# The compressed keys' first layer: 32 full-height products in place of 128 half-height ones

## The chip, the cores and the metric

The kernel runs on one core of a Trainium2 chip, all in float32, as one launch. The time is the device time of that launch in microseconds; lower is better. Five instruction queues run side by side and meet only at semaphores: TensorE (PE, matrix products and transposes into PSUM), VectorE (DVE), ScalarE (ACT), GpSimd (POOL) and SyncE (SP), of which SP only issues transfers here.

## What is computed

Two transformer blocks over 256 tokens of width 1024. The second block mixes a gated recurrence with a sparse attention, then runs a layer that picks 16 experts per head and token out of 16,384, and a gate. The change is in one piece of the sparse attention, the compressed keys and values: each of two key/value groups has 256 tokens of 64 features; blocks of 32 tokens, one every 16 tokens, are each flattened, given a position term and sent through a two-layer network.

```python
def compress(a, pe, w1, w2):          # a: groups x tokens x 64
    c = a.reshape(B, G, T // 16, 16, 64)
    blk = jnp.concatenate([c[:, :, j:j + n_cmp] for j in range(2)], axis=3)   # 15 blocks of 32 tokens
    blk = (blk + pe).reshape(B, G, n_cmp, 32 * 64)
    return jax.nn.gelu(blk @ w1) @ w2                                         # w1: 2048 x 64, w2: 64 x 64
kc = rmsnorm_2(compress(k_cmp, cmp_pe[0], cmp_w1[0], cmp_w2[0]), k_gain[0])
vc = compress(v_cmp, cmp_pe[1], cmp_w1[1], cmp_w2[1])
```

So the first layer is, for keys and for values (`kv`), a sum over 32 token places `j` of a 64x64 weight times the 15 tokens `16 m + j` of each group.

## The kernel before, in words

Everything stays in on-chip memory. Weights come from `wall` in 35 units of 2 MB, through a ring of three slots (`ring`); SP issues unit after unit, each when the unit that had its slot has been used (semaphore `unit_used`). One program for each engine is written out by hand, and the order in it is the order of execution. PE takes the units in the order `nq`, `nk`, `nv`, `hf`, `hq`, `cmp`, `hi`, `hg`, `wp0`, `wp1`, then the expert layer's. The function `project` runs a unit's products in eight parts and puts small steps of the attention and of the recurrence between the parts.

Around the change this is the order:

- PE (lines 679 to 771): the projections `nq`, `nk`, `nv`; two transposes of the normed keys and queries (`turn_nsa`); the projections `hf` and `hq` with the window attention of the first 128 tokens between their parts; then the unit `cmp` (line 740); then `project("hi")`, whose part 0 starts with `turn_keys` (line 752, eight transposes), part 1 with `within_chunks` (line 763), part 2 with `compressed` (lines 770 and 771, the second layer), part 4 with `turn_compressed`, part 6 with `compressed_scores`.
- DVE: `nsa_normed(t)` (line 1665) writes the normed, feature-major keys and values `nT3` for each half of the tokens; then four additions (line 1704) write `pe0` and `pe1`, the tokens with the position term of the block's first and second 16 places; then the attention's and the recurrence's steps, of which the last (line 1735) releases `turn_keys` through `recur_ready`.
- ACT: copies the projections out of PSUM (line 1080), does the exponentials of the recurrence (lines 1244 to 1249), then takes the first layer's sums out of PSUM through the gelu (lines 1254 and 1255), then moves the turned keys (line 1261).
- POOL: makes masks, issues the load of `post_g` (line 462) once block 1 is done, waits for `intra_moved` (line 471), and from there on gathers the experts' rows (line 489), 256 gathers of 1 MB.

In the unit `cmp` the group `g` is the half of the 128 partitions: features 0 to 63 of group 0 lie on partitions 0 to 63, those of group 1 on 64 to 127. Each product uses a 64x64 weight on one half of the array and 15 columns, each 16 tokens apart. There are 2 groups x 2 (`kv`) x 32 places = 128 products. A float32 product stands in the trace as two records, so these are 256.

PE's next instruction after the last of the 128 waits for `recur_ready`; ACT's next instruction waits for `unit_used` of `cmp`.

Of the kernel before, what the change touches and what calls it, by code (L numbers as in the profile page):

```python
# [19 lines left out]
ALU = mybir.AluOpType  # L20
ACT = mybir.ActivationFunctionType
AX = mybir.AxisListType.X

P = 128
SEQ = 256
# [50 lines left out]
def ring_slot(u):  # L76
# [15 lines left out]
        ("nq_g", 1), ("nk_g", 3), ("pe", 2 * CMP_LEN), ("cmp_w2", 2 * DH)]  # L92
COL_AT, NCOL = {}, 0
for _name, _width in COLS:
# [12 lines left out]
        "o_std", "nsa_sums", "nsa_std", "nsa_scaled", "nsa_turned", "nsa_normed", "cmp_in", "hid_made",  # L107
# [68 lines left out]
def two_blocks(nc, x, wall, cols, rows, lambdas, sub_keys, peer_uv, out):  # L176
    with ExitStack() as ctx:
# [42 lines left out]
        class at2:  # L220
# [16 lines left out]
            pe0, pe1 = sm[:, D:D + HALF], sm[:, D + HALF:2 * D]  # L237
# [26 lines left out]

        head_mask = small2[:, 1512:1520]
# [134 lines left out]
        def _(pool):  # L400
# [61 lines left out]
            pool.dma_start(post_g[:, :], rows[1:2, :].broadcast_to([P, D])).then_inc(s["rows_loaded"], 16)  # L462

# [31 lines left out]
        def _(pe):  # L495
# [570 lines left out]
        def _(act):  # L1066
# [184 lines left out]
            act.wait_ge(s["unit_used"], UNIT_AT["cmp"] + 1)  # L1251
            for g in range(NKV):
                half = slice(g * DH, (g + 1) * DH)
                nc.scalar.activation(hid_k[half, g * 16:g * 16 + NCMP], hid_psum[half, 0:NCMP], ACT.Gelu_apprx_tanh)
                ins = nc.scalar.activation(hid_v[half, :].rearrange("p (r m) -> p r m", r=REP)
# [886 lines left out]
```

## Time and profile before

| | us |
|---|---|
| median of 3 runs | 1183.0 |
| lowest, highest | 1182.2, 1183.18 |
| the profiled execution's own time | 1184.88 |
| its span in the profile | 1183.1 |
| mean granted TensorE clock in it | 0.974 of full |

The profile is one execution. Its views used here are the page (shares of the span, and the span in 40 slices), the chain of work that ended last (each step followed back to what released it), the timeline (instructions in order of time, neighbours merged, with the idle time before them and who ended it) and windows (busy time of each engine in a stretch, with the granted clock). The granted clock is 1.00 at 2.4 GHz and 0.50 at 1.2 GHz. The duration of a matmul record includes its way through the array, so what a row of records costs is read from the chain, where neighbours do not overlap.

### The profile page before, as it was taken

The page shows a single profiled execution, that of the slowest core. Times are in us where ns is not written, and L with a number is a line of the kernel's source. Part 1 is how long each engine was busy: PE and PEld are TensorE (multiplying, and loading weights), DVE is VectorE, ACT ScalarE, POOL GpSimd, SP SyncE. Part 2 cuts the span into 40 slices and gives each one's busy share as a digit, 9 for nine tenths or more (in the row PEclk, how much of TensorE's full clock was granted, in tenths as well). Part 3 has the DMA queues.
Part 4 walks back from the last instruction along what each step waited for, and adds up shares of the span by engine and source line. Part 5 has one row for each costly group of instructions (what it writes and reads, how often), then busy time and mean ns, then how long its engine had stood idle before and what let it go on. Part 6 is the DMA issues. An engine that isn't in the chain of part 4 may idle for free.

```text
span 1183.1 us, 9911 instructions
## 1 busy us (share of the span) xinstructions
PE 1036.0 (88%) x3363; PEld 558.0 (47%) x3363; DVE 641.5 (54%) x1446; ACT 390.8 (33%) x1019; POOL 310.2 (26%) x310
## 2 busy tenths in 40 slices
PE   6999899999999997988898997977699777777777
PEld 5887458544797554543344443322244222222223
DVE  2515345312540326877575655766776677667442
ACT  0133245211451123444433323423442432333222
POOL 3000000012000001244363433544354434444420
PEclk9999999999996998999999998999999999999999
DMA  7335322234531217699999999999999999999980
GB/s 276 143 142 213 142 99 115 88 139 165 195 143 72 107 71 284 219 369 423 420 422 420 421 421 422 420 419 420 421 393 420 421 419 420 421 420 420 420 346 18
DMA packets 43442, 346.96 MB, mean 293 GB/s; under 512 B 4832, under 2 KB 4960, under 8 KB 6016
## 3 DMA queue, kind: packets, MB, share of 16 engines
q0 software_dynamic: 37200, 269.63, 55.7%
q1 hardware_dynamic: 6192, 76.71, 17.1%
q8 instruction: 26, 0.43, 0.1%
q14 instruction: 24, 0.20, 0.0%
HBM read 345.27 MB, written 1.05 MB: 293 GB/s over the span
## 4 chain that ended last, share of the span: by engine, by line
PE 57%; DMA 30%; DVE 6%; ACT 4%; issue 2%; SPq 0%; POOL 0%; POOLq 0%; DVEq 0%
DMA spare<-in_peer_uv,small 17%; PE pp L940 15%; PE pp L524 7%; DMA gl<-in_peer_uv,small 7%; PE pp L552 5%; PE pp L548 4%; PE pp L534 3%; DMA ring<-in_wall 3%; PE pa L890 3%; DMA sm<-in_peer_uv,small 3%; PE pp L1032 2%; PE pp L659 2%; PE pp L679 2%; PE pp L637 2%; PE pa L740 2%
## 5 line engine op out<-in xcount | busy, mean ns | idle before, releaser
L1342 ACT ACTIVATE small<-small 128x2 f32<-128x2 f32 x128 | 26.0, 203 | 396.7 <-DVE small L1958 396.5
L940 PE MATMUL pp<-ga,diag 128*128 128x512 f32 x132 | 68.2, 641 | 34.3 <-ACT diag L1356 34.3
L1356 ACT ACTIVATE diag<-ident,small 128x128 f32<-128x128 f32 x256 | 88.7, 393 | 4.3
L940 PE MATMUL pp<-kT,diag 128*128 128x512 f32 x132 | 65.4, 618 | 27.3 <-ACT diag L1356 27.2
L940 PE MATMUL pp<-xc_rg,diag 128*128 128x512 f32 x132 | 65.5, 620 | 27.1 <-ACT diag L1356 27.1
L524 PE MATMUL pp<-hT,ring 128*128 128x256 f32 x384 | 85.8, 386 | 2.7 <-DMA ring<-in_wall 2.7
L524 PEld LDWEIGHTS pp<-hT,ring 128*128 128x128 f32 x384 | 74.6, 194 | 13.5 <-issue 3.0
L940 PE MATMUL pp<-tail,diag 128*128 128x512 f32 x116 | 56.6, 610 | 22.9 <-ACT diag L1356 22.3
L489 POOL DMA_INDIRECT xc_rg<-in_peer_uv,small x33 | 37.0, 1121 | 148.3 <-issue 77.8
L449 POOL IOTA tail<- 128x256 int32 x1 | 0.3, 341 | 248.3 <-DVE xs L1618 248.3
L1348 ACT ACTIVATE small<-small 128x1 f32<-128x1 f32 x256 | 61.4, 287 | 5.3
L940 PE MATMUL pp<-spare,diag 128*128 128x512 f32 x132 | 62.7, 598 | 0.0
L940 PE MATMUL pp<-ig,diag 128*128 128x512 f32 x132 | 62.4, 595 | 0.0
L940 PE MATMUL pp<-gl,diag 128*128 128x512 f32 x132 | 62.1, 592 | 0.0
L548 PE MATMUL pp<-ring,hT 128*128 128x512 f32 x128 | 61.3, 626 | 0.0
L940 PEld LDWEIGHTS pp<-ga,diag 128*128 128x128 f32 x132 | 24.2, 197 | 75.0 <-ACT diag L1356 54.1
L552 PE MATMUL pp<-hT,ring 128*128 128x256 f32 x256 | 58.1, 381 | 0.0
L1958 DVE CUSTOM_DVE_ANT_0 xc_rg<-xc_rg 128x1024 f32<-128x1024 f32 x33 | 40.4, 1225 | 30.2 <-DMA xc_rg<-in_peer_uv,small 30.0
L489 POOL DMA_INDIRECT ga<-in_peer_uv,small x33 | 37.5, 1136 | 71.3 <-PE pp L940 70.7
L1958 DVE CUSTOM_DVE_ANT_0 gl<-gl,xc_rg 128x1024 f32<-128x1024 f32 x33 | 40.4, 1224 | 27.5 <-DMA gl<-in_peer_uv,small 27.5
L1958 DVE CUSTOM_DVE_ANT_0 spare<-spare,xc_rg 128x1024 f32<-128x1024 f32 x33 | 40.5, 1226 | 27.3 <-DMA spare<-in_peer_uv,small 27.1
L890 PE MATMUL pa<-ring,hT 128*128 128x512 f32 (+1 forms) x112 | 52.4, 563 | 2.9 <-DMA ring<-in_wall 2.9
(384 smaller groups left out, 1888.3 us busy)
## 6 DMA issues: line engine op xcount, KB each, us to landing
ring<-in_wall SPq DMA_DIRECT2D x35, 2048.0 KB, 7.8
xs<-in_x SPq DMA_DIRECT2D x2, 512.0 KB, 3.8
post_g<-in_rows POOLq DMA_DIRECT2D x2, 512.0 KB, 8.7
lt<-in_sub_keys SPq DMA_DIRECT2D x1, 1024.0 KB, 6.4
out<-xs SPq DMA_DIRECT2D x4, 256.0 KB, 4.8
xc_rg<-in_peer_uv,small POOLq DMA_INDIRECT x33
gl<-in_peer_uv,small POOLq DMA_INDIRECT x33
ga<-in_peer_uv,small POOLq DMA_INDIRECT x33, 12.6
```

The lines of the kernel that those rows point to most:

```text
L489: nc.gpsimd.indirect_dma_start(out=rows_uv[page_of(g)], out_offset=None, in_=peer_uv, in_offset=bass.IndirectOffsetOnAxis(ap=experts[:, g: ...
L524: ins = nc.tensor.matmul(buf[:, c, :], w[:, k, c * P:(c + 1) * P], h3[:, k, :], start=(k == 0), stop=(k == KC - 1))
L534: ins = nc.tensor.matmul(buf[:, t, 0:width], h3[:, k, t * P:(t + 1) * P], w[:, k, 0:width], start=(k == 0), stop=(k == KC - 1))
L548: ins = nc.tensor.matmul(buf[:, t, :], h3[:, k, t * P:(t + 1) * P], w[:, k, :], start=(k == 0), stop=(k == KC - 1))
L552: ins = nc.tensor.matmul(flat[:, c, :], w[:, k, c * P:(c + 1) * P], h3[:, k, :], start=(k == 0), stop=(k == KC - 1))
L637: ins = nc.tensor.matmul(bufs[c][:, t, :], gl3[:, k, t * P:(t + 1) * P], wo[c][:, k, :], start=(k == 0), stop=False)
L890: ins = nc.tensor.matmul(to[:, a:b], h3[:, k, t * P:(t + 1) * P], w[:, k, a:b], start=(k == 0), stop=(k == KC - 1))
L940: ins = nc.tensor.matmul(acc[t][:, c, :], diag[:, n * P:(n + 1) * P], rows_uv[page_of(g)][:, D + c * HALF:D + (c + 1) * HALF], start=False ...
L1342: nc.scalar.activation(acts[:, at:at + BATCH], dots[:, at:at + BATCH], ACT.Gelu_apprx_tanh)\
L1348: ins = nc.scalar.activation(wk[:, g % LAG:g % LAG + 1], acts[:, g % LAG:g % LAG + 1], ACT.Copy, scale=probs[:, g:g + 1])
L1356: nc.scalar.activation(diag[:, n * P:(n + 1) * P], ident[:, :], ACT.Copy, scale=wk[:, g % LAG:g % LAG + 1]).then_inc(s["diag_made"], 1)
L1958: V.tensor_tensor_reduce(out=row_u, in0=row_u, in1=xn[t], scale=1.0, scalar=0.0, op0=ALU.mult, op1=ALU.add, accum_out=dots[:, g % LAG:g % ...
```

## The change

The contraction is made over 128 partitions: two neighbouring tokens at once. A new area `pairs` holds, for keys and for values, three planes of 256 columns. In plane 0 (group 0) the lower 64 partitions hold token n and the upper 64 token n + 1; plane 1 is the same for group 1; plane 2 holds the position term. A product takes a 128x64 weight (places 2j and 2j + 1) and 3 x 15 columns, one set of 15 from each plane: 2 (`kv`) x 16 = 32 products, which are 64 records. The sums of keys now lie on partitions 0 to 63 and those of values on 64 to 127, groups 0 and 1 in columns 0 to 29; the position term's share of the sum is in column 30, and ACT adds it as the bias of the gelu.

Two of the four quarters of the planes can be copied by DVE, since source and destination are on the same partitions. The other two move data between the partition halves; POOL issues a transfer for each, when both halves of `nT3` are there. In PE's program there is one more wait, for both transfers (`cmp_shifted`, 32).

```diff
 # POOL, behind the load of post_g and ahead of the waits for bias2_made and intra_moved
+            planes = at2.pairs.rearrange("p (v g n) -> p v g n", v=2, g=3)
+            low, high = slice(0, DH), slice(DH, 2 * DH)
+            pool.wait_ge(s["nsa_normed"], NT)
+            pool.dma_start(planes[low, :, 1, :], nT3[high, 6:8, :]).then_inc(s["cmp_shifted"], 16)
+            pool.dma_start(planes[high, :, 0, 0:SEQ - 1], nT3[low, 6:8, 1:SEQ]).then_inc(s["cmp_shifted"], 16)
 # PE
             pe.wait_ge(s["cmp_in"], 1)
             pe.wait_ge(s["ao_used"], 2)
-            for g in range(NKV):
-                half = slice(g * DH, (g + 1) * DH)
-                for kv in range(2):
-                    for j in range(CMP_LEN):
-                        src = (at2.pe0 if j < CMP_STRIDE else at2.pe1)[half, kv * SEQ:(kv + 1) * SEQ]
-                        n = (kv * CMP_LEN + j) * DH
-                        ins = nc.tensor.matmul(hid_psum[half, kv * 16:kv * 16 + NCMP],
-                                               w[half, n:n + DH],
-                                               src[:, j:j + CMP_STRIDE * (NCMP - 1) + 1:CMP_STRIDE],
-                                               start=(j == 0), stop=(j == CMP_LEN - 1))
+            pe.wait_ge(s["cmp_shifted"], 32)
+            planes = at2.pairs.rearrange("p (v g n) -> p v g n", v=2, g=3)
+            for kv in range(2):
+                for j in range(CMP_LEN // 2):
+                    n = (kv * CMP_LEN // 2 + j) * DH
+                    ins = nc.tensor.matmul(hid_psum[kv * DH:(kv + 1) * DH, 0:3 * NCMP], w[:, n:n + DH],
+                                           planes[:, kv, :, 2 * j:2 * j + CMP_STRIDE * (NCMP - 1) + 1:CMP_STRIDE],
+                                           start=(j == 0), stop=(j == CMP_LEN // 2 - 1))
             ins.then_inc(s["unit_used"], 1)
 # PE, second layer
-                nc.tensor.matmul(kc_psum, hid_k, col("cmp_w2", 0, DH), start=True, stop=True)
-                nc.tensor.matmul(vc_psum, hid_v, col("cmp_w2", DH, DH), start=True, stop=True)\
+                nc.tensor.matmul(kc_psum, hid_k[0:DH, :], col("cmp_w2", 0, DH)[0:DH, :], start=True, stop=True)
+                nc.tensor.matmul(vc_psum, hid_v[DH:2 * DH, :], col("cmp_w2", DH, DH)[DH:2 * DH, :], start=True, stop=True)\
 # ACT
             act.wait_ge(s["unit_used"], UNIT_AT["cmp"] + 1)
+            step(nc.scalar.activation(hid_bias, hid_psum[:, 2 * NCMP:2 * NCMP + 1], ACT.Copy))
+            nc.scalar.activation(hid_k[0:DH, :].rearrange("p (g m) -> p g m", g=NKV)[:, :, 0:NCMP],
+                                 hid_psum[0:DH, 0:2 * NCMP].rearrange("p (g m) -> p g m", g=NKV),
+                                 ACT.Gelu_apprx_tanh, bias=hid_bias[0:DH, :])
             for g in range(NKV):
-                half = slice(g * DH, (g + 1) * DH)
-                nc.scalar.activation(hid_k[half, g * 16:g * 16 + NCMP], hid_psum[half, 0:NCMP], ACT.Gelu_apprx_tanh)
-                ins = nc.scalar.activation(hid_v[half, :] ...
+                ins = nc.scalar.activation(hid_v[DH:2 * DH, :] ... , bias=hid_bias[DH:2 * DH, :])
 # DVE, ahead of the norms of nk
+            planes = at2.pairs.rearrange("p (v g n) -> p v g n", v=2, g=3)
+            step(V.memset(at2.pairs, 0.0))
+            V.tensor_copy(planes[:, :, 2, 0:CMP_LEN:2], col("pe", 0, CMP_LEN).rearrange("p (v j) -> p v j", v=2))
             V.memset(hid_k, 0.0)
 # DVE, behind nsa_normed(1)
-            for kv in range(2):
-                for n, dst in enumerate((at2.pe0, at2.pe1)):
-                    ins = V.tensor_tensor( ... 128 x 256, nT3 plus the position term ... )
-            step(ins, "cmp_in")
+            low, high = slice(0, DH), slice(DH, 2 * DH)
+            V.tensor_copy(planes[low, :, 0, :], nT3[low, 6:8, :])
+            step(V.tensor_copy(planes[high, :, 1, 0:SEQ - 1], nT3[high, 6:8, 1:SEQ]), "cmp_in")
```

The weights and the position term are laid out anew to match; the unit stays 2 MB.

## Rows read from the trace of the kernel before

**Rows 1.** The page: the span in 40 slices, and the chain's shares
```profile
DMA  7335322234531217699999999999999999999980
...
PE 57%; DMA 30%; DVE 6%; ACT 4%; issue 2%; SPq 0%; POOL 0%; POOLq 0%; DVEq 0%
```

**Rows 2.** The chain that ended last, 290 to 560: start us, us, what
```profile
345.58 23.10 PE pa L740 x256
368.67 1.90 PE pa L752 x8
370.57 3.41 PE pp L548 x4
373.99 1.18 PE pa L763 x32
375.16 1.91 PE pp L548 x4
...
445.49 7.77 DMA ring<-in_wall
```

**Rows 3.** Windows: busy us (records) of PE, PEld, DVE, ACT, POOL, granted clock
```profile
350.00:351.00 1.00, 1.00 (x15) 1.00 (x14) 1.00 (x2) 0.00 (x0) 0.00 (x0) 0.63 1.03 442
352.20:368.00 15.80, 15.80 (x155) 15.80 (x154) 0.00 (x0) 0.00 (x0) 0.00 (x0) 0.50 0.01 3
368.60:374.00 5.40, 5.40 (x15) 2.86 (x16) 0.00 (x0) 1.59 (x5) 0.00 (x0) 0.50 0.80 288
```

**Rows 4.** Timeline of ACT and DVE beside the unit cmp
```profile
347.39 1.28 ACT L1254 ACT_TABLE_LOAD   x1
350.89 1.22 DVE L1735 TENSOR_TENSOR xc_rg<-kT,xc_rg 128x1024 f32<-128x1024 f32 x1
368.71 0.18 ACT L1254 ACTIVATE small<-pa 64x15 f32<-64x15 f32 x1 [20.04 <-PE pa L740]
```

**Rows 5.** The same chain: short products and transposes at the full clock
```profile
321.26 0.87 PE pa L705 x8
...
384.96 1.71 PE pa L785 x16
```

**Rows 6.** Windows around idle stretches of PE, columns as in rows 3
```profile
144.70:148.40 3.70, 0.00 (x0) 0.00 (x0) 3.56 (x8) 0.00 (x0) 0.00 (x0) 1.00 0.00 0
148.94:152.35 3.41, 3.41 (x7) 1.57 (x6) 0.00 (x0) 0.60 (x1) 0.00 (x0) 0.51 0.00 0
436.30:437.60 1.30, 0.00 (x0) 0.00 (x0) 1.23 (x2) 0.00 (x0) 0.00 (x0) 1.00 0.00 0
449.00:452.60 3.60, 0.00 (x0) 0.00 (x0) 3.36 (x12) 1.94 (x4) 0.00 (x0) 1.00 0.86 369
453.40:459.50 6.10, 6.10 (x8) 2.48 (x9) 4.19 (x7) 0.00 (x0) 3.77 (x4) 0.50 0.48 150
467.80:470.40 2.60, 0.00 (x1) 0.01 (x1) 2.50 (x10) 2.13 (x9) 0.00 (x0) 0.87 1.02 425
470.40:473.00 2.60, 2.60 (x12) 2.60 (x13) 2.53 (x11) 1.93 (x3) 0.00 (x0) 0.50 0.71 296
```

**Rows 7.** Timeline of DVE and POOL ahead of the unit cmp
```profile
276.54 0.62 POOL L462 DMA_DIRECT2D post_g<-in_rows  x1 [4.27 <-DVE xs L1618]
283.82 0.17 DVE L1647 MEMSET small<- 128x128 f32 x1
300.82 0.96 DVE L1625 TENSOR_TENSOR sm<-nq 128x768 f32<-128x768 f32 x1 [16.67 <-ACT nq L1080]
315.61 1.43 DVE L1704 TENSOR_TENSOR sm<-vv,colt 128x256 f32<-128x256 f32 x4
```

**Rows 8.** Transfers: post_g from 270 to 300, then the gathers' stage as a window
```profile
post_g<-in_rows POOLq DMA_DIRECT2D x1, 512.0 KB, 4.9
520.00:1144.00 624.00, 514.22 (x1211) 217.77 (x1209) 413.66 (x1004) 224.57 (x675) 265.95 (x237) 0.98 1.01 419
```

**Rows 9.** Records of line 740: ns min/median/max, first and last start
```profile
L740 PE MATMUL pa<-sm,ring x256: 205/263/284, 345.5 to 368.4; 64*64 64x15 f32 x128
```

More of the change, by code:

```diff
@@ L91 @@
         ("mix_g", KC), ("ffn_g", KC), ("gate_g", KC), ("lb0", HG_HEADS), ("lb1", HG_HEADS), ("out2_g", KC),
-        ("nq_g", 1), ("nk_g", 3), ("pe", 2 * CMP_LEN), ("cmp_w2", 2 * DH)]
+        ("nq_g", 1), ("nk_g", 3), ("pe", CMP_LEN), ("cmp_w2", 2 * DH)]
 COL_AT, NCOL = {}, 0
@@ L106 @@
         "intra_moved", "intra_masked", "update_full", "states_made", "o_gated", "o_full", "o_moved", "o_sums",
-        "o_std", "nsa_sums", "nsa_std", "nsa_scaled", "nsa_turned", "nsa_normed", "cmp_in", "hid_made",
+        "o_std", "nsa_sums", "nsa_std", "nsa_scaled", "nsa_turned", "nsa_normed", "cmp_in", "cmp_shifted", "hid_made",
         "cmp_full", "cmp_sums", "cmp_std", "cmp_ready", "v_blocks_made", "cmp_turned", "cmpT_made", "cs_full", "cs_shifted",
@@ L236, in two_blocks @@
             nT = vv
-            pe0, pe1 = sm[:, D:D + HALF], sm[:, D + HALF:2 * D]
+            pairs = spare[:, HALF:HALF + 2 * 3 * SEQ]
             sc = [sm[:, 0:D], spare[:, 2 * D:3 * D], sm[:, D:2 * D], sm[:, 0:D], sm[:, D:2 * D], sm[:, 0:D]]
@@ L263, in two_blocks @@
         last_exp = small2[:, 1336:1352]
+        hid_bias = small2[:, 1448:1449]
         head_mask = small2[:, 1512:1520]
@@ L1251, in _ @@
             act.wait_ge(s["unit_used"], UNIT_AT["cmp"] + 1)
+            step(nc.scalar.activation(hid_bias, hid_psum[:, 2 * NCMP:2 * NCMP + 1], ACT.Copy))
+            nc.scalar.activation(hid_k[0:DH, :].rearrange("p (g m) -> p g m", g=NKV)[:, :, 0:NCMP],
+                                 hid_psum[0:DH, 0:2 * NCMP].rearrange("p (g m) -> p g m", g=NKV),
+                                 ACT.Gelu_apprx_tanh, bias=hid_bias[0:DH, :])
             for g in range(NKV):
-                half = slice(g * DH, (g + 1) * DH)
-                nc.scalar.activation(hid_k[half, g * 16:g * 16 + NCMP], hid_psum[half, 0:NCMP], ACT.Gelu_apprx_tanh)
-                ins = nc.scalar.activation(hid_v[half, :].rearrange("p (r m) -> p r m", r=REP)
+                ins = nc.scalar.activation(hid_v[DH:2 * DH, :].rearrange("p (r m) -> p r m", r=REP)
                                            [:, :, g * 16:g * 16 + NCMP],
-                                           hid_psum[half, 16:16 + NCMP].unsqueeze(1).broadcast_to([DH, REP, NCMP]),
-                                           ACT.Gelu_apprx_tanh)
+                                           hid_psum[DH:2 * DH, g * NCMP:(g + 1) * NCMP].unsqueeze(1)
+                                           .broadcast_to([DH, REP, NCMP]),
+                                           ACT.Gelu_apprx_tanh, bias=hid_bias[DH:2 * DH, :])
             ins.then_inc(s["hid_made"], 1)
@@ L2090, in lay_out @@
         elif name == "cmp":
-            w = np.asarray(i["cmp_w1_2"])[0].reshape(2, CMP_LEN, DH, DH).transpose(2, 0, 1, 3).reshape(DH, UNIT)
-            units.append(both(w))
+            w = np.asarray(i["cmp_w1_2"])[0].reshape(2, CMP_LEN // 2, 2, DH, DH).transpose(2, 3, 0, 1, 4)
+            units.append(padded([w.reshape(2 * DH, CMP_LEN * DH)]))
         elif name == "ple":
@@ L2114, in lay_out @@
         "nq_g": both(np.asarray(i["nsa_q_norm_2"]).T), "nk_g": both(np.asarray(i["nsa_k_norm_2"])[0].T),
-        "pe": both(np.asarray(i["cmp_pe_2"])[0].reshape(2 * CMP_LEN, DH).T),
+        "pe": np.asarray(i["cmp_pe_2"])[0].reshape(2, CMP_LEN // 2, 2, DH).transpose(2, 3, 0, 1).reshape(2 * DH, CMP_LEN),
         "cmp_w2": both(np.asarray(i["cmp_w2_2"])[0].transpose(1, 0, 2).reshape(DH, 2 * DH)),
```

5 lines of the change are left out of this document (removed).

## The prediction

> **What bounds the kernel now.** I read the page first: the chain that ended last is 57% PE and 30% transfers, and the row of the transfer engines shows two stages, one with them partly idle and, from about the seventeenth slice on, one with them full [rows 1]. Up to about 445 us PE sets the time; from about 520 us the gathers do, at 419 GB/s with the engines' share at 1.01 over 624 us [rows 8]. So a gain ahead of 445 us is worth something only if it moves the start of the gathers' stage, and a gain inside that stage would be worth little.
>
> Then I read the chain from 290 to 560 us. The products of the unit `cmp` stand in it as one piece of 23.10 us, 256 records, from 345.58 to 368.67, and everything that follows it up to 377 us is PE too, piece upon piece with no gap [rows 2]. So nothing else hides under these 23.10 us: they are on the path in full. The first transfer behind them in this part of the chain is at 445.49, a weight unit whose slot PE itself had to free, so it starts when PE gets there and moves with it [rows 2].
>
> Last I looked at the clock and at the neighbours in this stretch. The clock fell from 2.4 to 1.2 GHz inside the piece: the slice from 350 to 351 has a mean of 0.63, which puts the fall at 350.26 (0.26 at full, the rest at half), it was at half from 352.2 to 368, and it stayed there to 374 [rows 3]. PE was not idle before the fall; it was running these 64x64 products with 15 columns. And ACT had its gelu table loaded at 348.67 and then sat idle 20.04 us for PE, while DVE ended its last step of the recurrence (line 1735) at 350.89 + 1.22 = 352.11, 16.5 us before PE could use it [rows 4]. The reader is to see that the slack right behind the piece is large but not endless: the next PE instruction waits for exactly that DVE step.
>
> **The products, step by step.** First the price of an old record. From 345.58 to 350.26 PE ran at full clock, 4.7 us, and from there to 368.67 at half, 18.4 us, which is 9.2 us at full. Together 13.9 us at full clock for 256 records: 0.054 us each, and 0.109 at half.
>
> The new record has a 128x64 weight and 45 columns, at a stride of 16. No row shows it. From below, `within_chunks` (128x64 weights, 64 columns, two column halves in turn) took 1.18 us for 32, 0.037 each [rows 2]. From above, the scores of line 785 (128x128 weights, 32 columns) took 1.71 us for 16, 0.107 each, with twice the weight columns [rows 5]. I take 0.054, because the old records have the same 64 weight columns, and because twice the weight columns cost just twice as much (0.107), as if neither rows nor product columns counted at these sizes.
>
> The Trainium skill, TensorE: Matmul & The Clock Gate, section LDWEIGHTS, says that a weight load is paid by its columns and not by its height; its formula would give 53 ns for 64 columns, an estimate from that page, and so 3.4 us for 64 records. A price by rows used, as halving the height might suggest, would double it to 0.109.
>
> So 64 x 0.054 = 3.5 us, with 64 x 0.037 = 2.4 and 64 x 0.107 = 6.8 as ends; all at half clock, 7.0 from the middle price. The products start at 345.58, since `ao_used` and `cmp_in` are as before, and end at 349.1 (347.9 to 352.6).
>
> **What is late next.** `turn_keys` cannot start before DVE's line 1735 is done, at 352.11; with the 0.05 us that such a hand-over takes in the chain it starts at 352.2. PE then idles 3.1 us. It had started at 368.67. Gain so far 16.5 us. The upper end of the products' price (352.6 or so) would take 0.4 from it, so even a price twice mine is nearly covered by this wait. Nothing in DVE's or ACT's way to line 1735 is touched.
>
> **The clock behind it.** Before, the eight transposes took 1.90 us and the four products behind them 3.41, at half clock; the same at full clock took 0.87 [rows 5] and 1.91 [rows 2]. That is 1.03 + 1.50 = 2.5 us that come back if PE runs at full clock there. Does it? The idle stretches of PE give the answer: after 3.7 us idle (144.7 to 148.4), 3.6 us (449 to 452.6) and 2.6 us (467.8 to 470.4, where it fell within it) the clock was at half when or soon after work began again; after 1.3 us (436.3 to 437.6) it was not [rows 6]. The new idle of 3.1 us lies among those that cost the clock, so I take it that it falls. It came back at 152.35, 459.5 and 473.0, that is 3.9, 6.1 and 2.6 us after work had begun [rows 6]. In such a stretch half the time is lost: 1.3 to 3.05 us, with 1.95 in the middle.
>
> The Trainium skill, TensorE: Matmul & The Clock Gate, section HAM oscillation, says the same against this change: a burst of products followed by a wait starts its next burst throttled. By that rule the gain is the sum below; without it 1.95 us more. The trace's rows above agree with it for three idle stretches out of four.
>
> **The rest of the edits.** ACT's added copy and its wait, and a table load that now comes behind the wait for PE (1.28 us, and 0.18 for a small activation [rows 4]), then three gelus in place of four at about 0.2: about 2.3 us, so `hid_made` comes near 351.5, and near 355 if the products took 7.0. Its reader `compressed` follows turned keys, four products, `within_chunks` and four more: 352.2 + 0.87 + 1.91 + 1.18 + 1.91 = 358.1 at the earliest. ACT's next step, moving the turned keys, cannot start before 353.1. Covered; bare, it would cost at most that 2.3.
>
> DVE: clearing 1536 words, by 0.17 us for 128 words [rows 7] at most 12 x 0.17 = 2.0 us, lies with the small copy in the 16.67 us for which DVE waits for ACT before line 1625 [rows 7]: nothing. The four additions of 1.43 us [rows 7] become two copies of 64 partitions x 512 words, somewhere between half of that and all of it; behind them DVE waited for PE anyway. Nothing.
>
> POOL: two transfers of 128 KB, issued once `nsa_normed` is 2, at 314.35 + 1.22, or 315.6, where POOL has been idle since its load of `post_g` at 276.54 [rows 7]. Behind the new wait are queued only the mask step of the recurrence (which now is due near 357) and the gathers from 454.82 on; both have tens of microseconds. No row shows a move inside on-chip memory; POOL's load of four times the size, 512 KB, took 4.9 us to land [rows 8]. So both land by about 326 even if they queue behind each other, 19 us ahead of 345.58. Nothing, unless they take over 26 us from issue (345.58 less 315.6, less an idle that no one sees); then each further microsecond eats first the 3.1 us of PE's idle.
>
> SP: the slot of `cmp` is free 19.5 us earlier, so `wp0` comes earlier; no one waits for it. 192 fewer records have to be fetched and issued: not priced, it lies within the products' price.
>
> **The sum.** 16.5 + 2.5 - 1.95 = 17.1 us. Against the profiled execution's own time that is 1184.88 - 17.1 = 1167.8; against the median of the runs, 1183.0, it is **1165.9**. From 352 us on, every piece up to the gathers' first issue at about 455 hangs on PE or on what PE released, so I let the whole stage move; the gathers' stage then ends as much earlier, its length being bytes over rate.
>
> **The rivals.**
>
> 1. *The clock does not fall in the new idle.* It speaks for it that 3.1 us is near the shortest idle that cost the clock, and that the products before it have three times the columns. Gain 16.5 + 2.5 = 19.0: 1164.0. With the longest throttled stretch of the rows instead, 16.5 + 2.5 - 3.05 = 16.0: 1167.0, which I count with the forecast.
> 2. *The products are dear.* If the strided reading of three planes stops the records from overlapping, each costs its whole way through the array, 0.263 us in the old records' median [rows 9]: 64 x 0.263 = 16.8, PE ends at 362.4, the idle is gone, and the gain is 6.3, or 8.8 with the clock kept: 1174.2 to 1176.7. Against it: the old records read 15 columns at the same stride at 0.054.
> 3. *It does what it says and the end stays.* The gathers' stage is full with transfers, and if its start were held by something else than PE's progress, the 17 us would turn into idle time ahead of it: 1183. Against it: the chain from 345 to 445 has PE at every step that I list, and a weight load that PE triggers.
> 4. *Slower: the moved halves come late.* Each microsecond that the second transfer lands past 349 delays PE. Not faster than before from landing at 352.2 + 16.5 - 3.5, or about 365 us, on: 50 us after the issue, where four times the bytes took 4.9. At 60 us it would be 1193.
>
> **How the numbers follow.** Forecast with the clock falling 0.62, clock kept 0.22, dear products 0.09, absorbed 0.04, late transfers 0.03. The forecast's own range is 1164.0 to 1167.0. Later idle stretches of PE will meet the clock at another moment than now, each worth up to 3 us either way by rows 6; I widen by 1.5 below and 2.5 above: 1162.5 to 1169.5. That leaves out rivals 2 to 4 (0.16) and little of the rest. A difference of 0.2%, 2.4 us, is about what a measurement here can tell from none. Faster 0.93 (forecast, rivals 1 and 2), same 0.04, slower 0.03.
>
> **What would show it.** In the profile after: one piece of 64 records from about 345.5, some 3.5 us long (0.054 each; by rival 2, 17); then PE idle about 3 us with DVE's line for `recur_ready` as releaser; the transposes at about 352.2; a granted clock at half for 3 to 6 us around there (by rival 1, 1.00 throughout); ACT's gelus done before 352; both transfers landed before 330; POOL's first gather near 437.7 instead of 454.8. I am wrong if the first gather comes earlier by 17 us and the end does not, if the piece is over 7 us long, or if PE waits there for POOL's transfers.

## The result, and the profile after

| | before | after |
|---|---|---|
| median, us | 1183.07 (4 runs) | 1162.0 (4 runs) |
| lowest, highest | 1182.2, 1183.18 | 1161.0, 1163.97 |
| the profiled execution, its span | 1184.88, 1183.1 | 1161.04, 1159.3 |
| mean granted clock in it | 0.974 | 0.985 |

The ratio is 0.9818, with a 95% interval of 0.9804 to 0.9831. The kernel became 21.1 us faster; forecast were 17.1 us (1165.9), with a range down to 1162.5. The sign and the main mechanism were right, the size was 4.0 us short, and the time lies 0.5 us outside the range.

The page of the changed kernel, the 40 slices and the chain's shares, beside [rows 1]:

```profile
DMA  7435314244624326899999999999999999999980
...
PE 60%; DMA 27%; DVE 7%; ACT 4%; issue 2%; SPq 0%; POOL 0%; POOLq 0%; DVEq 0%
```

The chain that ended last, of the same kernel, beside [rows 2]:

```profile
346.25 1.03 ACT ig L1088
...
347.38 1.23 DVE xc_rg L1740
...
350.88 1.15 DVE xc_rg L1744
352.02 0.14 issue
352.16 1.07 PE pa L760 x8
353.22 1.72 PE pp L558 x4
354.94 1.08 PE pa L771 x32
356.02 1.91 PE pp L558 x4
...
426.48 7.54 DMA ring<-in_wall
```

The reader is to see that the piece of products is gone from the chain: it now passes through ACT and DVE, whose last step of the recurrence (now line 1744) releases the turned keys (now line 760) at 352.16. Before it was 368.67, so 16.5 us, as forecast. The pieces behind are short: transposes 1.07 where they were 1.90, products 1.72 where they were 3.41. That is the full clock, and `within_chunks` starts at 354.94 where it was 373.99: 19.05 us, and not the 17.1 of the forecast. The next weight wait is at 426.48, again 19.0 earlier.

The windows of the changed kernel (columns as in [rows 3]; behind the clock stand the transfer engines' share and GB/s): the piece, the idle behind it, what follows, and the stage from the first gather's issue to the last one's:

```profile
345.40:350.20 4.80, 4.80 (x65) 4.77 (x64) 2.82 (x3) 1.86 (x2) 0.00 (x0) 1.00 0.81 266
350.35:352.10 1.75, 0.00 (x1) 0.00 (x0) 1.66 (x2) 1.68 (x3) 0.00 (x0) 1.00 1.06 440
352.16:357.00 4.84, 4.84 (x47) 3.06 (x48) 0.00 (x0) 2.44 (x5) 0.20 (x1) 1.00 1.00 399
...
435.47:1117.36 681.89, 570.87 (x1415) 249.31 (x1414) 458.12 (x1121) 254.80 (x757) 284.81 (x256) 0.98 0.99 408
```

The clock did not fall. And the idle is 1.8 us, not 3.1, because the piece is longer than forecast. The timeline has it at 4.95 us, with 64 weight loads in 4.77, so 0.0745 us for each record:

```profile
345.40 4.77 PEld L749 LDWEIGHTS pa<-spare,ring 128*64 128x64 f32 x64 [0.33 <-issue]
345.40 4.95 PE L749 MATMUL pa<-spare,ring 128*64 128x45 f32 x64
...
350.39 0.17 ACT L1260 ACTIVATE small<-pa 128x1 f32<-128x1 f32 x1 [3.12 <-PE pa L749]
350.58 1.28 ACT L1261 ACT_TABLE_LOAD   x1
...
352.16 1.07 PE L760 MATMUL pa<-ident,xc_rg 128*128 128x128 f32 x8 [1.80 <-DVE xc_rg L1744]
352.17 0.50 ACT L1265 ACTIVATE small<-pa,small 64x60 f32<-64x60 f32 x2
...
356.80 1.38 POOL L481 TENSOR_SCALAR_AFFINE_SELECT gl<-gl 64x512 f32<-64x512 f32 x2 [39.73 <-ACT gl L1274]
...
435.47 1.47 POOL L499 DMA_INDIRECT xc_rg<-in_peer_uv,small  x1 [77.29 <-DVE small L1954]
```

The last line is the first gather: 19.35 us before the old one at 454.82. The stage of the gathers of the kernel before, and its stretch near the end, as windows:

```profile
454.82:1139.59 684.77, 571.67 (x1415) 250.11 (x1413) 458.00 (x1121) 254.64 (x757) 286.14 (x255) 0.98 0.99 406
1162.00:1167.00 5.00, 4.12 (x6) 1.90 (x7) 0.98 (x2) 1.28 (x1) 0.00 (x0) 0.66 0.00 0
```

With this the two profiled executions can be set against each other: 19.35 us ahead of the first gather, 684.77 - 681.89 = 2.9 in the gathers' stage, and from the last gather's issue to the end of the span (1183.1 - 1139.59) - (1159.3 - 1117.36) = 43.5 - 41.9 = 1.6, where the kernel before has a stretch at half clock. That makes 23.8 for this pair; by the medians it is 21.1. So two things were to be explained: the clock at 352 us, and some 2 us behind the first gather.

### The profile page after: what moved, and what is told of

Read it like the earlier page. It is cut to its first block, busy times and chain, and to the rows that moved or that the text cites. A ratio compares the mean times of both kernels' runs of the same rounds, so it can differ in the third digit from the quotient of the medians.

```text
span 1159.3 us, 9530 instructions
## 1 busy us (share of the span) xinstructions
PE 1012.9 (87%) x3171; PEld 536.9 (46%) x3171; DVE 642.1 (55%) x1446; ACT 391.4 (34%) x1019; POOL 310.1 (27%) x312
## 4 chain that ended last, share of the span: by engine, by line
PE 60%; DMA 27%; DVE 7%; ACT 4%; issue 2%; SPq 0%; POOL 0%; POOLq 0%; DVEq 0%
PE pp L948 19%; DMA spare<-in_peer_uv,small 14%; PE pp L534 7%; DMA gl<-in_peer_uv,small 7%; PE pp L558 4%; DMA ig<-in_peer_uv,small 4%; PE pp L562 4%; PE pa L898 3%; PE pp L544 3%; DMA ring<-in_wall 3%; PE pp L1040 2%; PE pp L669 2%; PE pp L689 2%; PE pp L647 2%; PE pp L872 2%
```

## The experiments

Each kernel is the changed one with the edit shown, unless said otherwise. The kernel before ran beside them, with medians of 1183.84, 1184.21, 1183.21 and 1184.1 us in the four groups. Of its 42 runs there, 29 took 1181.7 to 1184.6 us and 13 took 1186.7 to 1190.5, with none between; the four runs in the table above have none of the longer kind.

### What prices a record, and what the idle does to the clock

Four kernels change only the operands of the 32 products.

```diff
 # e1_contiguous
-   planes[:, kv, :, 2 * j:2 * j + CMP_STRIDE * (NCMP - 1) + 1:CMP_STRIDE],
+   at2.pairs[:, kv * 3 * SEQ + 2 * j:kv * 3 * SEQ + 2 * j + 3 * NCMP],
 # e2_columns15 (e3_columns30: 2 in place of the 1)
-   ins = nc.tensor.matmul(hid_psum[..., 0:3 * NCMP], w[:, n:n + DH], planes[:, kv, :, ...],
+   ins = nc.tensor.matmul(hid_psum[..., 0:(3 if j == 0 else 1) * NCMP], w[:, n:n + DH],
+                          planes[:, kv, 0:3 if j == 0 else 1, ...],
 # e4_rows64
-   w[:, n:n + DH], planes[:, kv, :, ...],
+   w[0:DH, n:n + DH], planes[0:DH, kv, :, ...],
```

`e1_contiguous` forms the sums of other tokens, `e2_columns15` leaves out group 1 and the position term in all products but the first of each sum, `e3_columns30` the position term there, and `e4_rows64` leaves out every second token place.

**e1_contiguous.** 

> The changed kernel with 45 neighbouring columns in each product in place of 3 x 15 at a stride of 16 (so the sums are of other tokens). In the changed kernel a record cost 0.0745 us where 0.054 was forecast. Theory S (strided reading sets the price of a record): the price falls to 0.054, the 64 records end near 348.9, and PE idles about 3.2 us before line 1744's result. Theory C (product columns count as such) and theory H (the 128 rows count): it stays 0.0745, end 350.2. On the clock: if an idle of about 3 us is what costs it, as the prediction had it, then by theory S the clock is at half somewhere from 350 to 358 in most runs and the time is 1 to 3 us above the changed kernel's 1162; else it is the same within 1 us.

**e2_columns15.** 

> The changed kernel with 15 columns (group 0 alone) in all but the first product of each sum, still 128 rows high. Theory S and theory C: a record costs about 0.054 as the old ones did with 15 columns. Theory H: it stays at 0.0745.

**e3_columns30.** 

> The changed kernel with 30 columns (both groups, no position term) in all but the first product of each sum. Theory C, linear between 0.054 at 15 and 0.0745 at 45: 0.064. Theory S, reading at the pace of 0.0745 / 45 = 1.66 ns a column with a floor of 0.054 for the weights: 30 x 1.66 = 0.050, so the floor, 0.054. Theory H: 0.0745.

**e4_rows64.** 

> The changed kernel with products over the lower 64 partitions only (one token in place of two), 45 strided columns as before. Theory H: a record falls to 0.054. Theories S and C: it stays at 0.0745.

Measured: 1163.4 us (4 runs, ratio 0.9812, 0.9773 to 0.9851), and in one run each 1162.07, 1164.87 and 1166.05. The weight loads of the piece in `e1_contiguous`, by line (ns min/median/max, first and last start):

```profile
L749 PEld LDWEIGHTS pa<-spare,ring x64: 133/138/138, 344.6 to 348.1; 128*64 128x64 f32 x64
```

The same in `e4_rows64`:

```profile
L749 PEld LDWEIGHTS pa<-spare,ring x64: 129/149/224, 344.7 to 349.4; 64*64 64x64 f32 x64
```

First start to last start over 63 gives 0.056 us for 45 columns that lie side by side, 0.057 for 15 strided ones (344.0 to 347.6; 0.056 for 30), and 0.075 for 45 strided ones on half the rows, the same as on all rows. So the rows do not count for the pace, and 45 columns alone do not either; 45 columns at a stride of 16 do. The three strided forms fit two limits of which the larger sets the pace: the weights' 0.056, and the reading of the strided columns, which passes it somewhere between 30 and 45 columns. The 45 columns also come from three planes, 30 from two and the contiguous ones from a single run; no run separates the stride from the number of planes.

The Trainium skill, TensorE: Matmul & The Clock Gate, section LDWEIGHTS, has the load paid by its columns and not by its height. These runs agree: with 15 strided columns a record took 0.054 us at 64 rows (the kernel before) and 0.057 at 128 (`e2_columns15`). Its 53 ns are near that, but they are not the price of the piece here.

The three cheap pieces are 1.2 us shorter and leave PE idle for 3.0 us, and in all three the clock fell. The idle and a window behind it in `e1_contiguous`:

```profile
351.38 1.06 PE L760 MATMUL pa<-ident,xc_rg 128*128 128x128 f32 x8 [3.03 <-DVE xc_rg L1744]
```

```profile
352.00:356.00 4.00, 4.00 (x17) 1.46 (x16) 0.00 (x0) 1.02 (x1) 0.00 (x0) 0.57 1.01 434
```

Where it fell, read from windows of 0.5 us, differs: at 352.4 in `e1_contiguous`, 1.0 us after work had begun again; at 351.1 in `e3_columns30`, in the middle of the idle; at 348.2 in `e2_columns15`, only 0.4 us into it. In `e4_rows64` it fell at 349.0, while PE was still running the piece, which ended at 349.8:

```profile
345.00:349.00 4.00, 4.00 (x57) 4.00 (x56) 2.32 (x3) 1.56 (x2) 0.00 (x0) 1.00 0.84 262
349.05:349.75 0.70, 0.70 (x8) 0.60 (x6) 0.70 (x1) 0.00 (x0) 0.00 (x0) 0.50 1.09 468
```

So that fall can't be put down to the idle of 1.65 us behind it. It differs from the changed kernel by the rows alone, and is like the fall in the kernel before, whose products have 64 rows too.

So the forecast's rule held for the idle that it assumed, in the profiles of `e1_contiguous` and `e3_columns30` (and in `e2_columns15`, if 0.4 us of idle were what did it), and the dearer record spared the kernel that idle. The section HAM oscillation of the same page, by which a wait after a burst has the next burst start throttled, agrees with `e2_columns15` and `e3_columns30`, whose transposes ran at half clock from their start; in `e1_contiguous` they started at full. It describes longer waits than the changed kernel's 1.8 us, behind which the next burst started at 1.00.

### How far the start is passed on, and whether the kept clock was luck

```diff
 # e5_twice: every product twice
-                for j in range(CMP_LEN // 2):
+                for i in range(CMP_LEN):
+                    j = i % (CMP_LEN // 2)
 # e7_fill: turned keys one part of the projection later
-            project("hi", {0: turn_keys, 1: within_chunks, 2: compressed, 4: turn_compressed, 6: compressed_scores})
+            project("hi", {1: turn_keys, 2: lambda: (within_chunks(), compressed()), 4: turn_compressed,
+                           6: compressed_scores})
 # e8_four_products: the first and the last place of each sum
-                for j in range(CMP_LEN // 2):
+                for j in (0, CMP_LEN // 2 - 1):
```

`e6_after` is the changed kernel itself once more.

**e5_twice.** 

> The changed kernel with its 32 products made twice over (the sums double), 128 records at 0.0745. They end at about 345.4 + 9.5 = 354.9 in place of 350.2, so the turned keys start at 355.0 in place of 352.2, 2.8 us later. Theory 1 (what moves the start of the turned keys moves the end one for one, the gathers' stage only follows): the time is 2.8 us above that of the unchanged copy of the changed kernel run beside it, give or take the clock, 1 us. Theory 2 (part of a shift is absorbed in the gathers' stage): clearly less than 2, near 0.

**e6_after.** 

> The changed kernel once more, beside the others. Theory A (the gain is 19.05 us up to the gathers, and the rest up to 21.1 is the clock meeting later idle stretches at another moment): the time scatters by 1 to 3 us from run to run, the second profile has its half-clock stretches elsewhere, and in some profile PE's idle of 1.8 us costs the clock after all. Theory B (something in the gathers' stage is really faster): the stage from the first gather's issue to the last is 681.9 us again, and 2 to 3 us shorter than before's 684.8 in every profile of a kernel with the change.

**e7_fill.** 

> The changed kernel with the turned keys and what follows moved one part later in the projection of hi, so that four products of 1.72 us in sum stand in PE's idle of 1.8 us ahead of them. Theory 1 (PE is on the path from 352 us to the gathers, and the order of these small steps costs no one a wait): 1.7 us less than the unchanged copy. Rival (the small steps' readers, DVE and ACT, are then late, above all the scores of the compressed keys): 0 to 1 us less, with a new idle of PE between 355 and 380.

**e8_four_products.** 

> The changed kernel with 4 of its 32 products (the first and the last of each sum; the rest of the first layer is left out). PE has nothing from about 345.8 to 352.2, 6.3 us. By the chain the turned keys start at 352.2 as before, since DVE's step sets it. Theory of the clock (an idle of 3 us or more costs it, for 3 to 7 us from some moment in it): half clock in every run behind it and a time of 1 to 3.4 us above the unchanged copy, though 60 records less are to be run. Rival (the clock has nothing to do with it): the same time.

`e6_after` took 1162.74 us (5 runs, ratio 0.9825, 0.9801 to 0.9849): three runs at 1161.9 to 1162.7 and two at 1167.8 and 1168.0. Its profile is of one of the latter. The turned keys came at 352.52 and the clock did not fall there: the second profile in which an idle of 1.8 us kept it. But it fell later, beside the first gathers:

```profile
434.00:467.00 33.00, 26.86 (x93) 18.29 (x94) 21.73 (x56) 11.59 (x33) 6.49 (x7) 0.74 0.53 207
```

In the profile after, the same window has 0.92 and 239 GB/s. The stage of the gathers was 686.8 us long against 681.9. So the same program takes 1161 or 1168 us, and what differs most between the two profiles up to the gathers' steady stretch is the clock from 434 to 467 us. The kernel before does the same, with 13 of its 42 runs some 6 us above the rest. Taken over all nine runs of the changed kernel its median is 1162.7.

`e5_twice` took 1167.88 (1165.04 to 1170.51), ratio 0.9852 (0.9826 to 0.9878). Its chain:

```profile
345.25 9.93 PE pa L750 x128
355.18 1.02 PE pa L761 x8
```

The turned keys start 3.0 us later than in the profile after. Median against median the kernel is 5.1 us above `e6_after`, but both have runs of two kinds, in other proportions: the lower two, 1165.04 and 1165.57, lie 2.9 us above the mean of the lower three of `e6_after`, and the upper two, 1170.19 and 1170.51, 2.4 above the mean of its upper two. So nearly all of the later start reaches the end, in as far as four runs can show it. The profiled one of the upper runs has its clock at half from 455 to 466 us, as `e6_after` had from 453 to 467. Within the 9.93 us the clock was at full, and `e9_before_half` below shows that this is not a matter of course:

```profile
345.30:355.10 9.80, 9.80 (x128) 9.70 (x128) 4.63 (x4) 1.73 (x2) 0.00 (x0) 1.00 0.60 216
```

`e8_four_products` has almost no piece, and took 1164.22 (1162.23 to 1167.95), no less than the kernel that does all products (1162.74 beside it, with overlapping runs). PE idled for 6.2 us, the clock fell, and the chain has each piece at its dear price:

```profile
352.39 1.94 PE pa L760 x8
354.33 3.41 PE pp L558 x4
357.75 1.15 PE pa L771 x32
```

`e7_fill` puts products where the idle was (the piece from 345.89, 4.88 us long, then four products, then the transposes at 352.69), with the clock at full, and its first gather is at 433.91, 1.6 us ahead of the profile after. Expected was that this reaches the end; it did not: 1163.99 (1162.63 to 1164.75), against 1162.74 of `e6_after`. In its profile the gathers' stage is 685.0 us long, with the clock at half beside the first gathers:

```profile
449.00:461.00 12.00, 11.71 (x53) 10.47 (x52) 7.56 (x28) 4.94 (x10) 0.00 (x0) 0.57 0.24 99
```

So `e5_twice`, `e6_after` and `e7_fill` point to the same place: what is gained by 435 us can be lost again right behind it.

### The old form of the products with half of them

This is the kernel before, with every second place `j`.

```diff
-                    for j in range(CMP_LEN):
+                    for j in range(0, CMP_LEN, 2):
...
-                                               start=(j == 0), stop=(j == CMP_LEN - 1))
+                                               start=(j == 0), stop=(j == CMP_LEN - 2))
```

**e9_before_half.** 

> The kernel before with every second place left out of its first layer: 64 products of the old form, 128 records, nothing else changed (no transfers, no planes, no bias). Theory 1 (all of the gain is PE's time in this piece, down to the wait for DVE's line 1735): 128 x 0.054 = 7.0 us, so the piece ends near 352.5, the turned keys start near 352.6, and the time is that of the changed kernel within 1 to 3 us, the more if the clock falls in the piece as it did before (at 350.26). Rival (some of the gain is in other parts of the change, or its transfers, copies and bias cost something): over 3 us away from it.

**e10_before.** 

> The kernel before once more, for a second profile. Theory A (from the first gather on both kernels differ only by where the clock falls): its stage from the first gather's issue to the last lies between 681.9 and 687 us, as in the profiles with the change, longer where PE is at half clock behind the first gathers. Theory B (the stage is really shorter with the change): it is 684.8 again while the clock's rows differ.

`e9_before_half` took 1171.26 us (5 runs, 1168.64 to 1176.14), ratio 0.9894 (0.9858 to 0.9931), far above what its first theory expected, and where its rival had it (over 3 us away from the changed kernel). Its chain and a window of it:

```profile
345.52 9.46 PE pa L740 x128
354.99 1.90 PE pa L752 x8
356.89 3.41 PE pp L548 x4
```

```profile
350.00:355.00 5.00, 5.00 (x51) 4.96 (x50) 2.06 (x2) 0.00 (x0) 0.00 (x0) 0.52 0.46 190
```

It has as many records as `e5_twice`, starts them at nearly the same time (345.5 and 345.2), has no idle ahead and none behind, and its clock fell at about 350.2, 4.7 us into them, and stayed at half to 360.4; that of `e5_twice` stayed at 1.00. One has 64 rows and 15 columns, the other 128 rows and 45. `e4_rows64` above, with 64 rows and 45 columns, fell within its piece as well, 4.3 us into it, and so did all three profiles of the kernel before, 4.1 to 4.7 us into theirs. In none of the seven profiles with a full piece of 128 rows and 45 strided columns did the clock fall while the products ran. So the products of half the height take PE's clock down while PE is busy, and those of full height do not; that it is the rows and not the 15 columns rests on the one profile of `e4_rows64`. Without that fall the 128 records of `e9_before_half` would have taken 128 x 0.054 = 6.9 us and ended at 352.4, an estimate from the old record's price.

The windows account for the rest, and leave nothing for the rival, a cost or a gain in another part of the change. Against the profile after, the first gather is 441.13 - 435.47 = 5.7 us later (2.8 for the turned keys and 2.5 for the half clock up to `within_chunks` are most of that), the gathers' stage is 685.0 - 681.9 = 3.1 longer and the end behind it 1.5 longer, 43.4 against 41.9: 10.2 together, the difference of the two spans.

The same price tells how the gain of the change divides. At full clock throughout, the 256 old records would have taken 13.9 us in place of 23.1 and ended at 359.5, an estimate. So of the 16.5 us up to the turned keys 9.2 are the half clock that the old products brought on themselves, and of the 19.0 us up to `within_chunks` 11.7; the smaller number of records alone is worth the other 7.3.

`e10_before` is the kernel before, once more: 1183.06 us, stage of the gathers 685.2, from the last gather to the end 41.9 us.

### The clock beside the first gathers

Seven products of 128x128 by 512 columns, whose result no one reads, stand in two waits of PE near 431 and 445 us in the changed kernel. They write a bank of PSUM that is overwritten later. (The number in the call counts records; 8 and 5 make four and three products.)

```diff
+            def keep_busy(bank, n):
+                for _ in range(n // 2 + n % 2):
+                    nc.tensor.matmul(bank, ident[:, :], hT[:, 0:HALF], start=True, stop=True)
...
             pe.wait_ge(s["pscore_moved"], 1)
+            keep_busy(pp[:, 0, 0], 8)
             query_part(2, range(KC))
             pe.wait_ge(s["pscore_moved"], 2)
             att_scores(3)
+            keep_busy(pp[:, 0, 1], 5)
```

`e11_busy` and `e14_after_busy` are the changed kernel with this, `e12_fill_busy` is `e7_fill` with it, and `e13_before_busy` the kernel before with it.

**e11_busy.** 

> The changed kernel with products that no one reads (identity by 512 columns, 8 and 6 records) in two of PE's idle stretches: in the wait for the weights near 430 to 434 and in the wait for the exponentials near 448 to 450.5. Theory (the clock behind these idles costs 2.6 to 3 us at 434 and 5 us where it falls at 453): no half clock from 434 to 467, the first gathers' stage at its short length, and a time at or 1 to 3 us below the good runs of the changed kernel (1161 to 1163), without runs near 1168. Rival (the stage's length is set by transfers, not by PE's clock there): the same scatter and median as the changed kernel, 1162 to 1163.

**e12_fill_busy.** 

> The same unread products, on top of the order that fills PE's idle ahead of the turned keys (whose own 2 us gain up to the first gather did not reach the end: its profile had half clock from 449 to 461). Theory (it was the clock that took it): 1.5 to 2 us below the run with the unread products alone, 1158 to 1161. Rival (the gathers' stage absorbs it): the same as that run.

**e13_before_busy.** 

> The kernel before, with the same seven unread products in two waits of PE behind the last expert weights (four and three of 128x128 by 512 columns), so that the clock is kept at about 434 to 467 us after the first gathers' start. Theory A (the part of the gain past the 19.05 us that the first gather moves is the state of the clock beside the first gathers): the gathers' stage of this kernel is as long as that of the changed kernel with the same products, 679.7 us within 1, so it takes 1180 to 1181, some 2.5 us under the kernel before, and 19 us above the changed kernel with the products. Theory B (the changed kernel's stage is shorter for another reason, such as 192 records fewer to fetch or the order of the transfers): the stage stays at 682 or more and the time at 1182.5 to 1184, 21 us above the changed kernel with the products.

**e14_after_busy.** 

> The changed kernel with the same seven unread products, once more and beside the kernel before with them, on one chip. Both theories: 1159.5 to 1163 with no run above 1164. The difference to the kernel before with the products is what tells the theories apart: 18.5 to 19.5 us by theory A, 20.5 to 21.5 by theory B.

| | median (runs) | lowest, highest | ratio to before, interval |
|---|---|---|---|
| `e11_busy` | 1161.71 (5) | 1159.57, 1162.83 | 0.9805, 0.9776 to 0.9835 |
| `e14_after_busy` | 1159.82 (5) | 1158.57, 1161.96 | 0.9794, 0.9769 to 0.9819 |
| `e12_fill_busy` | 1157.49 (5) | 1155.45, 1159.86 | 0.9766, 0.9735 to 0.9798 |
| `e13_before_busy` | 1180.45 (12) | 1178.2, 1182.53 | 0.9961, 0.9943 to 0.9979 |

In ten runs of the changed kernel with the products none came near 1168, and in twelve of the kernel before none is above 1182.53, where 5 of the 17 runs without them are at 1188.8 to 1190.4. The kernel before gains 3.65 us by them in its median; against the median of those of its runs that are not of the longer kind, 1183.48, it is 3.0. Windows of `e13_before_busy`, the gathers' stage and the rest behind it:

```profile
455.29:1136.71 681.42, 572.53 (x1420) 250.24 (x1418) 458.39 (x1121) 254.82 (x757) 284.07 (x255) 0.98 0.99 408
...
1136.71:1180.10 43.39, 31.38 (x72) 13.25 (x72) 12.79 (x20) 10.57 (x26) 0.94 (x1) 0.96 0.24 97
```

And of `e14_after_busy`, beside the first gathers, then the same two:

```profile
434.00:470.00 36.00, 33.34 (x134) 19.13 (x132) 28.38 (x71) 12.96 (x37) 11.30 (x10) 1.00 0.70 268
...
437.24:1117.95 680.71, 571.61 (x1420) 249.37 (x1418) 458.05 (x1121) 254.81 (x757) 282.91 (x256) 0.98 0.99 409
...
1117.95:1159.80 41.85, 29.89 (x72) 12.60 (x72) 12.79 (x20) 10.56 (x25) 0.94 (x1) 1.00 0.25 102
```

With the clock kept there, the stages of the old and the new kernel are 681.4 and 680.7 us long (`e11_busy` 679.7): the difference of 2.9 is nearly gone, and both are shorter than the 684.8 and 685.2 of the kernel before. All sixteen profiles together say the same, with some overlap. Without half clock from 425 to 480 us the stage took 679.7 to 681.4 us (four profiles, old and new kernel); with one stretch of 6.8 us at half clock 681.9 to 685.2 (seven); with 10 to 17 us 684.8 to 687.0 (five).

The forecasts of the last two runs come out mixed. The time of `e13_before_busy`, 1180.45, is theory A's, and theory B's 682 or more and 1182.5 or more did not come; but its stage of 681.4 is also longer than A's 679.7 within 1. And the difference of the two medians, 20.6 us, lies in theory B's 20.5 to 21.5 and not in A's 18.5 to 19.5. The two profiles differ by 18.05 at the first gather, 0.7 in the stage and 1.5 in the last 42 us, 20.3 together. The 18.05 are 1.3 less than in the first pair, since `e14_after_busy` had 3.4 us of half clock at 418.9, and the 1.5 are half clock in the last stretch of `e13_before_busy`. Such stretches come and go from run to run. With all ten runs of the changed kernel with the products (median 1161.6) the difference is 18.8. So these runs show that the clock beside the first gathers costs time in both kernels; whether the change is worth 19 us or 21 without that, they do not settle.

`e12_fill_busy` beats both kernels: its median is 25.7 us under that of the kernel before (1183.21), and 4.2 under `e11_busy` beside it (expected were 1.5 to 2). The same program as `e11_busy` took 1159.82 as `e14_after_busy` in another group, 2.3 above `e12_fill_busy`; so part of the 4.2 may be scatter, and how much is not settled. Its chain has no idle ahead of the turned keys:

```profile
346.52 4.88 PE pa L749 x64
351.40 1.91 PE pp L558 x4
353.31 0.89 PE pa L760 x8
```

`e11_busy` also shows that the clock at 352 us was kept in part by luck. Up to there it is the changed kernel, with the same idle to the hundredth, and in its profile the clock was at half from 352.1 to 355.5, 3.4 us:

```profile
351.22 1.13 PE L760 MATMUL pa<-ident,xc_rg 128*128 128x128 f32 x8 [1.80 <-DVE xc_rg L1750]
```

In the profile after, in `e6_after` and in `e14_after_busy` the idle of 1.8 us kept the clock; here it did not.

## Why the prediction was partly right, step by step

**What bounds the kernel: right.** All 23.1 us stood on the path, and the gathers' stage started as much earlier as PE got there: 19.35 us at the first gather. The end moved by all of it, and `e5_twice` has most of a later start reach the end, so rival 3 (absorbed) is out.

**The products: mis-sized.** "I take 0.054, because the old records have the same 64 weight columns, and because twice the weight columns cost just twice as much (0.107), as if neither rows nor product columns counted": rows did not, weight columns did (0.056), but 45 strided columns cost 0.0745, within the bounds of 0.037 to 0.107. The piece took 4.95 us where 3.5 was forecast. On the path this cost nothing, since DVE was late anyway. Rival 2 with 0.263 is out.

**What is late next: right.** Turned keys at 352.16 (forecast 352.2), released by DVE's last step of the recurrence, 16.5 us gained.

**The clock behind it: the step that failed.** "The new idle of 3.1 us lies among those that cost the clock, so I take it that it falls." The idle was 1.8 us, for the record's price above, and in both profiles of the unchanged kernel the clock stayed at full. The term of -1.95 us was 0, and rival 1 came about, with its 19.0 us. `e1_contiguous`, `e2_columns15` and `e3_columns30` restore the idle of 3 us and with it the half clock: the rule that I took from the rows fits them, and its input, the idle, came from a price that I had set too low. A shorter idle did not make the clock safe, though: with 1.80 us it was kept in three profiles out of four, and lost in `e11_busy`. So part of the 1.95 us is luck. One of the rows had also been read short: the idle taken as 3.6 us (449 to 452.6) lasted 4.46, to 453.39. The stretches that cost the clock in the kernel before were 2.7, 3.8 and 4.5 us long, the one that kept it 1.4; 3.1 still lies among the former, and 1.8 lay in the gap, for which the rows had no answer. What was missing in the working is that link: the range for the price (0.037 to 0.107) was used for the path, where it did not matter, and not for the length of the idle, where it decided.

**The rest of the edits: right.** ACT's second gelu ended at 352.67 and its reader came at 357.87. POOL's mask step came at 356.80. The two transfers were issued at 315.77 and 316.47; the transfers from 310 to 330 us of the changed kernel, KB each and us to landing:

```profile
spare<-vv POOLq DMA_DIRECT2D x1, 128.0 KB, 2.4
spare<-vv POOLq DMA_DIRECT2D x1, 127.5 KB, 2.3
```

So they were there by 319, 26 us early, and rival 4 is out. (The prediction's bound of 26 us from issue should have been 30, 345.58 less 315.6; nothing hangs on it.)

**The sum.** 16.5 + 2.5 = 19.0 makes 1164.0. The other 2 us are in "I let the whole stage move; the gathers' stage then ends as much earlier, its length being bytes over rate". That step failed too: the length is not only bytes over rate. In the pair of profiles the stage was 2.9 us shorter (684.8 to 681.9) and the last 42 us 1.6 shorter, with other stretches at half clock. The range had 1.5 us below for this; it was 2, on top of the clock at 352 us, and only both together lead out of the range. `e11_busy`, `e13_before_busy` and `e14_after_busy` show that keeping the clock beside the first gathers is worth 3.65 us to the old kernel, and that the runs near 1168 are gone from the new one. How much of these 2 us belongs to the change is open: the nine runs of the changed kernel have a median of 1162.7, inside the range, and its other profile has a stage of 686.8.

What stays open: which half clock costs how much. `e10_before` and the profile after have one beside the first gather each, of about the same length, and their stages are 685.2 and 681.9 us long. Also open is why some runs have a half clock in their last 42 us, which are then 43.4 to 43.5 us long in place of 41.8 to 42.0: two of the three profiles of the kernel before, `e9_before_half`, but `e4_rows64` and `e5_twice` as well, so it is not the old kernel's alone.

## What to carry to other kernels

A product's pace has several limits, and a new form must be priced by each: the weight's columns, and the moving operand with its stride; the half height of the old form had bought nothing, and its products took the clock down with them. Where a change ends in "then the engine idles", the length of that idle is a number that needs its own bounds, because the clock behind can depend on it: here the piece that is 1.2 us longer (1162.0) took no more in all than the shorter one (`e1_contiguous`, 1163.4). A wait of TensorE that can't be removed can be filled, with real products from behind it or with unread ones: one step moved and seven unread products took the kernel from 1162 to 1157.5 us. And a time that comes in two kinds, some 6 us apart, has to be read by kind before two medians are compared.

## What was not expected of the hardware

- The clock fell within uninterrupted products when these were 64 rows high: 4.1 to 4.7 us into the piece in five profiles (the kernel before three times, `e9_before_half`, `e4_rows64`), and not in as many products of 128 rows with 45 columns (`e5_twice`, 9.93 us at 1.00). With 64 rows and 45 columns it fell (`e4_rows64`), so the number of columns does not explain it.
- An idle of 1.80 us kept the clock in three profiles of the same form and lost it in a fourth (`e11_busy`); it was lost at 3.0 (three kernels) and at 6.2, in one profile each.
- 45 float32 columns at a stride of 16 elements, from three planes, take 0.0745 us a record where contiguous ones take 0.056, which is the pace of the 64 weight columns.
- PE's clock at the start of a stage that is full with transfers for 600 us still moves its end: with a mean of 1.00 at the first gathers it was 680 to 681 us long, with 0.92 from 434 to 467 us 681.9, with 0.74 there 686.8.
